# The second even projection of a two-layer diffusion trunk: its activations computed from x in SBUF, in place of stored halves read back

## What is computed

```python
def modulate(x, g, shift, scale):
    return rmsnorm(x, g) * (1.0 + scale) + shift

h_l = modulate(x, norm1_g[layer], sh1, sc1)          # latent tokens
h_c = modulate(xc, norm1_g[layer], csh1, csc1)       # context tokens
# even layer: EVEN_SPLITS = 512 (qa), 512 (ka), 512 (va), 512 (qb), 128 (kb), 128 (vb)
o_l, o_c = even_mixer(h_l @ ev_w_in[i], h_c @ ev_w_in[i], ...)
# inside: q and k of each head are rms-normalized, and rotated by rope_2d
```

## Time and profile before

| | |
|---|---|
| median of three runs | 4344.25 us |
| lowest and highest | 4341.76 and 4353.84 us |
| the profiled execution | 4365.38 us, of which 4363.6 us lie between its first and last instruction |
| TensorE busy in it | 3736.8 us (86%) |
| VectorE, ScalarE, GpSimd busy | 1943.0, 1161.6, 204.0 us |
| mean granted TensorE clock | 0.917 of full |
| moved by DMA | 354.39 MB, mean 81 GB/s |

### The profile page before, as it was taken

The page is one execution under the profiler, slowest core; times in us unless marked ns, Lnnn a source line. Parts: engine busy times, 40 slices in busy tenths (PEclk is TensorE's granted clock), DMA queues, the critical chain, the costliest instruction groups (busy, mean ns, idle before and its releaser), DMA issues. The chain is left out here.

```text
span 4363.6 us, 46998 instructions
## 1 busy us (share of the span) xinstructions
PE 3736.8 (86%) x17932; PEld 2950.0 (68%) x17932; DVE 1943.0 (45%) x2659; ACT 1161.6 (27%) x1897; POOL 204.0 (5%) x185
## 2 busy tenths in 40 slices
PE   5658778979686999999978878699889887999998
PEld 2246666668575888888866767566566665888887
DVE  4667436568526333333345354333234325333333
ACT  3543213346312111111114333333222312111111
POOL 0023111000002000000001000000000001000000
PEclk7879889989797999999998988699989998999999
DMA  6724445352200111111104433312254211111111
GB/s 249 262 92 139 159 136 109 79 122 67 75 20 27 39 39 36 38 38 36 39 17 155 148 109 106 100 44 65 50 103 95 78 29 36 56 46 43 48 54 64
DMA packets 404638, 354.39 MB, mean 81 GB/s; under 512 B 102005, under 2 KB 343429, under 8 KB 399365
## 3 DMA queue, kind: packets, MB, share of 16 engines
q1 hardware_dynamic: 404485, 352.35, 28.0%
HBM read 264.61 MB, written 87.69 MB: 81 GB/s over the span
## 5 line engine op out<-in xcount | busy, mean ns | idle before, releaser
L1961 DVE SCALAR_TENSOR_TENSOR xT<-ps,mods,xT 128x1024 f32<-128x1024 f32 (+1 forms) x216 | 213.1, 1014 | 650.1 <-PE ps L2029 481.0
L2029 PE MATMUL ps<-m_hh,m_w1h 128*128 128x512 f32 x1280 | 354.8, 375 | 66.6 <-DVE m_hl L2083 66.6
L2029 PE MATMUL ps<-m_hh,m_w1l 128*128 128x512 f32 x1280 | 353.7, 374 | 0.0
L2029 PE MATMUL ps<-m_gh,m_w2h 128*128 128x512 f32 x1280 | 350.8, 371 | 3.0 <-DVE m_gl L2098 2.8
L2029 PE MATMUL ps<-m_hl,m_w1h 128*128 128x512 f32 x1280 | 353.2, 374 | 0.0
L2029 PE MATMUL ps<-m_gl,m_w2h 128*128 128x512 f32 x1280 | 349.1, 370 | 0.0
L2029 PE MATMUL ps<-m_gh,m_w2l 128*128 128x512 f32 x1280 | 348.9, 370 | 0.0
L2094 DVE TENSOR_TENSOR m_g<-m_g 128x1280 f32<-128x1280 f32 (+1 forms) x64 | 87.0, 1359 | 544.6 <-ACT m_g L2065 544.6
L2029 PEld LDWEIGHTS ps<-m_hh,m_w1h 128*128 128x128 f32 x1280 | 225.1, 190 | 118.2 <-issue 41.0
L2065 ACT ACTIVATE m_g<-ps 128x1280 f32<-128x1280 f32 (+1 forms) x64 | 72.5, 1134 | 759.3 <-PE ps L2029 759.3
L2029 PEld LDWEIGHTS ps<-m_gh,m_w2h 128*128 128x128 f32 x1280 | 222.8, 188 | 50.7 <-DVE m_gl L2098 8.9
(11 more groups left out here) (297 smaller groups left out, 7163.2 us busy)
## 6 DMA issues: line engine op xcount, KB each, us to landing
aw<-in_ada_w SPq DMA_DIRECT2D x24, 2048.0 KB, 9.0
m_raw<-in_mlp_w SPq DMA_DIRECT2D x64, 512.0 KB, 4.1
m_raw<-in_mlp_w SPq DMA_DIRECT2D x128, 256.0 KB, 2.8
qkC<-pc_stage SPq DMA_DIRECT2D x72, 192.0 KB, 2.3
hT<-pa_hb SPq DMA_DIRECT2D x10, 1024.0 KB, 5.3
qkA<-pa_stage SPq DMA_DIRECT2D x20, 512.0 KB, 3.2
pb_hb<-hT SPq DMA_DIRECT2D x10, 1024.0 KB, 5.1
ab_k<-qkB SPq DMA_DIRECT2D x32, 320.0 KB, 7.2
```

Of the source, the lines that this page charges most:

```text
L1961: ins = k.nc.vector.scalar_tensor_tensor(out=x, in0=ps, scalar=k.mods[:, layer, gate, bass.ds(n, 1), w], in1=x, op0=ALU.mult, op1=ALU.add)
L2029: mm = pe.matmul(k.ps[:, SB * (e % 2) + b, 0:n], w[:, e % 2, f], m[:, f, c0:c0 + n], start=(f == 0 and x == 0), stop=(f == nf - 1 and x == 2))
```

## The change

The call of `project` for pb passes `keeps_h=True`.

```diff
         project(k, "pb", 0, ev, 1024, 1280, [
             Unit(512, 512, 8, ins["swa_q_g"][0], HD ** -0.5, True, k.qkB, 0),
             Unit(1024, 256, 2, ins["swa_k_g"][0], 1.0, True, k.qkB, 8, v=128, v_dst=k.vB),
-            Unit(0, 512, v=512, v_dst=k.vA)], keeps_h=False)
+            Unit(0, 512, v=512, v_dst=k.vA)], keeps_h=True)
```

## The result

Over eight runs of each kernel the median is 4363.44 us against 4344.5 us before. The ratio of the runs is **1.0036, with a 95% interval of 1.0025 to 1.0048**: 15.6 us slower, between 10.9 and 20.9.

What follows compares the result with a forecast made beforehand. TensorE was taken to bound pb's tiles, VectorE and weight slices its start. Start 3.2 us plus seven tile periods 4.5 us gave +7.7 us: 4344.25 to 4352.0 us, range 4343 to 4363.

Steps and rivals of the forecast that it cites:

- TensorE bounds the tiles and the loads are hidden there: pb's ten tiles: TensorE busy 15.00 of 15.00 us, so removing ten 1 MB loads gains no tile time.
- The collision: pb, tiles 0 to 7: VectorE's L645 waits for GpSimd's L680 (`base` of tile t + 2), 2.09 us more.
- Rival 1: pb: L645 goes before L680, which waits under cover; start costs 1.1 us, tiles nothing: 4345.4 us; chance 0.09.
- The loop: pb tile, `turn` of u0 through L630 and L651 to the next `turn`: 1.55 us slack, period +0.64 us.
- The way over ScalarE: pb tile: copy, eight L552 and cut of `h` end at T + 7.11 against T + 7.20; decides nothing.
- The start: pb before the tiles: L630 1.1 us late, then 2.09 in the head chain; cut of u2's weights +3.2 us.
- The 4.0: Start of pb: us taken for u1's weight slices, between bounds of 2.8 and 7.6; equals 262 GB/s.
- Rival 2: pb: TensorE's clock falls in the tiles, up to 4376 us; partial fall or longer slow start likelier, about 4362; chance 0.12.
- Rival 3: Start of pb: without loads u1's slices take 2.8 us, u0's eighth comes 2 us sooner; total 4348.8 us; chance 0.08.
- The step from pb to the whole: Whole kernel: engine time added inside pb carries over unchanged to the median of the runs, +7.7 us.
- slower by over 0.3%: Whole kernel: outcome slower by more than 13 us, most of the clock's fall and part of the unseen; chance 0.14.

Runs made afterwards that it cites:

- no_store: Changed kernel without the stores of the halves in pb and the waits on them; pb 189.4 us, ratio 1.0026 against the kernel before.
- collide_only: Kernel before, still loading the halves, plus only GpSimd's L680 in pb, written to an unread buffer; pb 186.3 us, ratio 1.0012.
- base_early: Changed kernel with GpSimd's base of tile t + 2 in pb moved ahead of the rotated product of u0; pb 182.6 us, ratio 1.0010.
- base_late: Changed kernel with GpSimd's base of tile t + 2 in pb moved behind the rotated product of u1; pb 186.9 us, ratio 1.0020.
- loads_split: Kernel before, pb loading the halves, with GpSimd's base in pa made in two halves at separate places; pa 173.9 us, pb 180.9, ratio 0.9967.
- null_before: Kernel before, unchanged, run again; pb 180.9 us, ratio 0.9994.

## Why the prediction was right, and where it was off

- **TensorE bounds the tiles and the loads are hidden there.** Right. The stores in their place are hidden too (no_store).
- **The collision, 2.09 us on L645 in tiles 0 to 7.** Right in place, size and count: 2.79 against 0.69, in the changed kernel and with the GpSimd instruction alone (collide_only). Rival 1, VectorE first, did not occur in any of these tiles.
- **The loop has 1.55 us of slack, so 0.54 us of wait and 0.1 after it, +0.64 a tile, +4.5 in all.** Right: 15.60 against 15.58 forecast, +4.4. The `turn` comes 0.55 us later and what follows it 0.1; that the profile counts only 0.39 of the 0.55 as waiting was not foreseen. base_early shows the slack from the other side: 0.83 us fit.
- **The way over ScalarE ends just ahead and decides nothing.** Right; collide_only has the same period without it.
- **The start, +3.2.** The mis-sized term: the cut of u2 came 4.0 us later. The eighth slice of u0 was cut after 14.96 us (forecast 14.99), the weights of u1 took 4.65 us rather than 4.0, and from them to L630 it was 4.64 rather than 4.37; the collision was 2.04. The 4.0 had no row behind it: 262 GB/s is not "a little more" than the 137 of the tiles but nearly twice as much, and only the bounds of 2.8 and 7.6 were sound. Of the 4.0 us by which the cut is late, 3.8 reach the first `turn`. With this the sum for pb is 8.4 against 7.7.
- **Rival 2, the clock.** Did not occur: 1.00 in the tiles. Nor was the slow stretch in the start longer: behind the pause ahead of u2 the slow products (0.63 us each, where later ones take 0.39) go from 477.27 to 482.56, and went from 475.16 to 480.87 before, though the pause has doubled.
- **Rival 3, the loads held the start.** Did not occur in its own terms: u1's slices took 4.65 us, not under 3, and the eighth of u0 was no sooner than in pa. Against the kernel before the slices came 2.5 us sooner, but what was set in the loads' place costs more.
- **The step from pb to the whole.** This is what fell short. I took for granted that what is added in pb is what the runs show. They show 15.6 and 11.7 us for 8.4, and the points of the other variants that are slower (base_early 4.3 for 1.3 us, base_late 8.7 for 5.6, no_store 11.3 for 8.1) lie some 3 us above their pb as well, while collide_only's does not (5.2 for 5.0). Each interval alone but the first holds the value of pb. Three things speak for chance: loads_split, which doesn't recompute in pb, lies 2.9 us above its phases too (in its profile pa and pb together are 17.3 us shorter, in time it is 14.4), null_before, the very same program, came out 2.6 us below before, and the stretch behind pb is no longer in the profiles with recomputing. A cost of some 3 us behind pb isn't excluded, and the cause of the excess stays open. I also gave "slower by over 0.3%" only 0.14, with a forecast 5 us below that line and phases around pb whose spread I had not looked at.

## What to carry to other kernels

Before work is put on an idle engine, lay its instruction beside the ones that run at that moment on VectorE: here GpSimd was busy for 5% of the span, and the place of one of its instructions was worth 7.0 of 8.4 us, while the recomputing itself cost 1.3. A stretch in which VectorE reads PSUM or a single SBUF operand is the place for it, and cutting it to the length of that stretch made pa, whose tiles VectorE's chain paces, 17 us shorter. When an instruction is moved, follow its consumers as well: moved later it left one loop and closed another.

## What the runs showed of the hardware

- Ahead it is said that the engines meet only at semaphores. L680 and L645 share none, and yet L645 took 2.79 us beside L680 and 0.69 without, in collide_only too, where L680's result goes nowhere; it ended 0.54 us behind L680 in tiles 1 to 7. L630 (one operand in SBUF) and L631 (one in SBUF, one in PSUM) beside a half of it (1.28 us) kept their 0.68 us. L637, L645 and L620, which became longer, have both operands in SBUF.
- Where VectorE was first, GpSimd's instruction was the longer one: in the start of the changed pb an L680 that starts 0.16 us behind an L620 (451.87 and 451.71) took 2.74 us, and the one ahead of it, with VectorE idle, 2.34.
- A wait of TensorE that the profile counts as 0.39 us cost 0.66 us of period: 0.16 of lost overlap with the product ahead of it and 0.1 in the eight transpositions, which take 1.11 instead of 1.00 us, come on top.
- The attention ab took 231.9 and 243.5 us in two executions of the same program, with 170 and 124 matmuls in its first 60 us.
